# Hybrid mixer of a float32 transformer on one core: heads in pairs, attention inside the projections

## The reference, cut to what matters

```python
h = x @ w_in                                  # 1024 -> 2816
qa, ka, va, qr, kr, vr, gr = split(h)         # 512,128,128,512,512,512,512
qa, ka = apply_rope(qa), apply_rope(ka)       # 8 query heads, 2 key heads of 64
y_attn = sliding_window_sink_attention(qa, ka, va, sinks)   # window 128, blocks of 128
qr, kr = pair_rotation(qr), pair_rotation(kr) * HEAD_DIM ** -0.5
y_ret = multiscale_retention(qr, kr, vr, gr)  # 8 heads: (q k' * decay) v, group norm, silu(gr) gate
return concatenate([y_attn, y_ret]) @ w_out   # 1024 -> 1024
```

## Time and profile before

| | |
|---|---|
| median of three runs | 2790.81 us |
| profiled execution, its own time | 2790.5 us |
| its span | 2788.7 us |
| mean granted TensorE clock | 0.919 |
| busy share of the span: PE, DVE, ACT, POOL | 86%, 34%, 29%, 6% |
| chain that ended last, by engine | PE 79%, DVE 7%, DMA 6%, issue 4%, ACT 3% |
| HBM | 252 GB/s over the span |

### The profile page before, as it was taken

The page is one execution under the profiler, slowest core; times in us unless marked ns, Lnnn a source line. Parts: engine busy times, 40 slices in busy tenths (PEclk is TensorE's granted clock), DMA queues, the critical chain, the costliest instruction groups (busy, mean ns, idle before and its releaser), DMA issues.

```text
span 2788.7 us, 39503 instructions
## 1 busy us (share of the span) xinstructions
PE 2404.5 (86%) x14190; PEld 1708.1 (61%) x14191; DVE 956.3 (34%) x1687; ACT 821.8 (29%) x1357; POOL 166.6 (6%) x274
## 2 busy tenths in 40 slices
PE   5899858888886968888888699998899899988997
PEld 2445523333333963333333699877899899867997
DVE  0223030000002750000000554565554554746554
ACT  1221111111111421111111344443443543443444
POOL 0000001111111001111111000000000000000000
PEclk8899979999998989999999799987999999968999
DMA  9511859999998527999998755422346446222442
GB/s 395 203 58 61 311 216 427 389 427 428 427 409 348 185 106 303 428 427 424 420 415 350 251 175 164 151 77 88 132 156 214 136 154 197 91 90 92 160 150 84
DMA packets 301584, 677.58 MB, mean 243 GB/s; under 512 B 14808, under 2 KB 209368, under 8 KB 259472
## 3 DMA queue, kind: packets, MB, share of 16 engines
q1 hardware_dynamic: 289440, 659.05, 61.2%
q0 software_dynamic: 10720, 8.45, 0.9%
q10 hardware_dynamic: 1296, 8.32, 0.8%
HBM read 682.29 MB, written 20.19 MB: 252 GB/s over the span
## 4 chain that ended last, share of the span: by engine, by line
PE 79%; DVE 7%; DMA 6%; issue 4%; ACT 3%; SPq 1%; POOLq 0%; DVEq 0%; ACTq 0%; POOL 0%
PE ps L1628 28%; PE ps L1078 14%; PE ps L1098 8%; PE ps L1811 5%; DMA ring<-in_moe_w_up 3%; DMA ring<-in_w_mod 3%; DVE arena L1291 1%; PE ps L1089 1%; PE ps L688 1%; PE ps L1079 1%; ACT arena L1155 1%; PE ps L1445 1%; PE ps L1447 1%; PE ps L1446 1%; PE ps L458 1%
## 5 line engine op out<-in xcount | busy, mean ns | idle before, releaser
L1628 PE MATMUL ps<-XS,WS 128*128 128x256 f32 x4224 | 521.0, 287 | 22.8 <-DVE XS L439 22.8
L1628 PEld LDWEIGHTS ps<-XS,WS 128*128 128x128 f32 x4224 | 518.1, 194 | 26.6 <-DVE XS L439 26.4
L1078 PE MATMUL ps<-ring,arena 128*64 128x512 f32 x1040 | 466.4, 602 | 61.0 <-issue 58.1
L1079 PE MATMUL ps<-ring,arena 128*64 128x512 f32 x1040 | 467.9, 603 | 0.0
L1613 DVE TENSOR_TENSOR WS<-ring,WS 128x1024 fp32r<-128x1024 f32 (+1 forms) x276 | 329.5, 1194 | 299.2 <-ACT WS L1608 299.0
L1608 ACT CAST WS<-ring 128x1024 fp32r<-128x1024 f32 (+1 forms) x276 | 282.0, 1023 | 442.9 <-PE ps L1628 420.4
L1078 PEld LDWEIGHTS ps<-ring,arena 128*64 128x64 f32 x1040 | 139.8, 139 | 351.4 <-issue 351.4
L1291 DVE TENSOR_TENSOR arena<-arena,ps 64x512 f32<-64x512 f32 x65 | 44.8, 690 | 851.9 <-ACT arena L1155 851.9
L1098 PE MATMUL ps<-ring,arena 128*64 128x512 f32 x520 | 269.0, 666 | 39.6 <-DVE arena L1294 39.6
L1099 PE MATMUL ps<-ring,arena 128*64 128x512 f32 x520 | 270.8, 670 | 0.0
L1628 PE MATMUL ps<-HS,WS 128*128 128x256 f32 x2112 | 262.2, 285 | 0.0
(11 more groups left out here) (272 smaller groups left out, 2712.3 us busy)
## 6 DMA issues: line engine op xcount, KB each, us to landing
ring<-in_moe_w_gate SPq DMA_DIRECT2D x64, 2048.0 KB, 16.5
ring<-in_moe_w_up SPq DMA_DIRECT2D x64, 2048.0 KB
ring<-in_moe_w_down SPq DMA_DIRECT2D x64, 2048.0 KB, 18.5
ring<-in_ffn_w_gu SPq DMA_DIRECT2D x90, 1024.0 KB, 7.6
ring<-in_w_mod SPq DMA_DIRECT2D x24, 2048.0 KB, 13.5
ring<-in_ffn_w_down SPq DMA_DIRECT2D x32, 1408.0 KB, 6.3
ring<-in_w_in SPq DMA_DIRECT2D x10, 2048.0 KB, 7.7
ring<-in_conv_w_in SPq DMA_DIRECT2D x6, 2048.0 KB, 18.0
```

What stands on the lines that cost most here:

```text
L1078: pe.matmul(ps[0:CAP, 0, :], x, gate[:, j, c, :], start=k == 0, stop=k == KD - 1)
L1079: mm = pe.matmul(ps[CAP:P, 0, :], x, up[:, j, c, :], start=k == 0, stop=k == KD - 1)
L1628: mm = L.eng.matmul(out_ap, weights[:, i, :], moving[:, j, k, :], start=k == 0 and weights is wh and j == 0, stop=k == total - 1 and weigh ...
```

## The change

- Heads lie in pairs on 128 partitions: `QA`, `QT`, `KR` are four tiles of 128x256 each, `KA` holds each key head on both halves. A rotation ends in one addition of 128x256; for `ka` it ends in four of 64x256.
- `ka` is projected first, straight from `XT`; `qa` 0 to 3 follow.
- Attention works on four pairs, inside the steps of the projections. At step i of 21: scores of pair i//4 at i = 3, 7, 11, 15; VectorE's masking there; exponentials at the step after; normalising at i = 5, 9, 13, 17; transposes at 6, 10, 14, 18; probabilities by values at 7, 11, 15, 19. The result is rounded and split straight from PSUM into `YS`.
- Masking, maxima and scaling work on both heads at once, with broadcast operands.
- Gates are copied, and one Silu of 128x1024 follows.
- An output unit is now half the k tiles by 256 output columns: units 20 to 23 are attention's half, 24 to 27 (`B_UNIT`) retention's. Attention's half is computed between the pairs of retention. All eight output tiles stay in four PSUM banks until the end.
- The four reciprocals and the normalising of retention are laced with that half. Retention's k tiles 4 and 5 come as eight output tiles each, then 6 and 7 together.
- The residual is added two tiles at a time. The LayerNorm behind the mixer uses banks 2 and 3, and now splits the feed-forward's unit 3 itself.

TensorE's new order, with the helpers cut:

```diff
+                def scores(p):
+                    L.wait(self.rotated, p + 2)
+                    if p:
+                        L.wait(self.p_kept, p)
+                    for cols, keys in ((slice(0, P), slice(0, P)), (slice(P, 3 * P), slice(0, TL))):
+                        for j in range(2):
+                            queries = slice(0, P) if cols.start == 0 else slice(P, TL)
+                            mm = pe.matmul(self.pair_tile(j)[:, cols], QA[self.heads(j), p, queries], KA[self.heads(j), p // 2, keys],
+                                           start=True, stop=True)
+                    L.inc(mm, self.scores)
...
+                for i in range(5, self.STEPS):
+                    if i < self.VALUE_STEP:
+                        project(i)
+                        turn(i - 1)
+                    elif i < self.GATE_STEP:
+                        retention_values(i - self.VALUE_STEP)
+                        if i == self.VALUE_STEP:
+                            turn(12)
+                    else:
+                        gate(i - self.GATE_STEP)
+                    if i % 4 == 2:
+                        turn_probs(i // 4 - 1)
+                    if i % 4 == 3:
+                        finish(i // 4 - 1)
+                        if i // 4 < self.PAIRS:
+                            scores(i // 4)
...
+                r_scores(0)
+                window_half(0)
+                r_scores(1)
+                r_finish(0)
+                window_half(1)
+                r_scores(2)
+                r_finish(1)
+                mean(0)
+                window_half(2)
+                r_scores(3)
+                r_finish(2)
+                mean(1)
+                variance(0)
+                window_half(3)
+                r_finish(3)
+                mean(2)
+                variance(1)
+                mean(3)
+                variance(2)
+                for k in (4, 5):
+                    L.wait(self.y_split, k + 1)
+                    for m in range(KD):
+                        L.wait(self.w_split, B_UNIT + m // 2 + 1)
+                        y_products(m, k)
+                    if k == 4:
+                        variance(3)
+                for m in range(KD):
+                    for k in (6, 7):
+                        L.wait(self.y_split, k + 1)
+                        mm = y_products(m, k)
```

VectorE's new order:

```diff
+                for i in range(self.STEPS):
+                    if 1 <= i <= self.VALUE_STEP:
+                        rotate(i - 1)
+                    if i % 4 == 3 and i >= 7:
+                        split_out(i // 4 - 1)
+                    if i % 4 == 3 and i // 4 < self.PAIRS:
+                        mask_scores(i // 4)
+                    if i % 4 == 1 and 5 <= i <= 17:
+                        normalise(i // 4 - 1)
+                    if i < self.VALUE_STEP:
+                        if i:
+                            self.split_weights(L, self.unit_of(i) + UNITS)
+                    else:
+                        self.split_weights(L, GATE_UNIT + i - self.VALUE_STEP)
...
+                decay(3)
+                centre(1)
+                gate(0)
+                add_eps(0)
+                self.split_weights(L, B_UNIT + 2)
+                centre(2)
+                gate(1)
+                scale(0)
+                add_eps(1)
+                centre(3)
+                gate(2)
+                scale(1)
+                self.split_weights(L, B_UNIT + 3)
+                split_gated(0)
+                add_eps(2)
+                gate(3)
+                scale(2)
+                split_gated(1)
+                add_eps(3)
+                scale(3)
+                split_gated(2)
+                split_gated(3)
```

More of the change, by code:

```diff
@@ L146 @@
 ACT_PER_LAYER = 0
-DVE_PER_LAYER = 108
+DVE_PER_LAYER = 75
 SPLITS_PER_LAYER = 2 * FFN_UNITS + MIXER_UNITS
@@ L1816, in pe, with project @@
-                stream = [[XS[:, x, k, :] for x in range(2)] for k in range(KD)]
+                    L.inc(mm, self.w_used)
+                def project(i):
+                    if i >= 2:
+                        L.wait(self.raw, i - 1)
+                    if i:
+                        products(self.unit_of(i), self.tile(i), self.x_split if i == 1 else None)
+                        return
+                    slot_ready(L, self.first + 1)
+                    wv = self.weights(1, 256)
+                    for k in range(KD):
+                        L.wait(self.x_high, k + 1)
+                        mm = pe.matmul(self.tile(i), wv[:, k, 0:P], XT[:, k, 0:TL], start=k == 0, stop=k == KD - 1)
+                    L.inc(mm, self.key_tile)
@@ L1818, in turn @@
                 def turn(i):
                     L.wait(self.raw, i + 1)
[L1821 to L1825, removed]
+                    if i:
+                        L.wait(self.rotated, i)
+                    L.inc(pe.matmul(self.turned_tile(), TURN_A if i < 5 else TURN_R, RAW[i % 2], start=True, stop=True), self.turned)
@@ L1848, in pe, with retention_values @@
[L1848 to L1857, removed]
-                    else:
-                        products(self.unit_of(i), ps[:, i % 2, 0:TL], stream, range(KD), self.x_split if i == 0 else None)
+                def retention_values(q):
+                    if q == 0:
+                        L.wait(self.values_kept, 2)
+                    u = VALUE_UNIT + q
+                    L.wait(self.w_split, u + 1)
+                    high_part, low_part = self.parts(u)
+                    for t in range(2):
+                        for i in range(2):
+                            k = 2 * q + i
+                            for weights, x in ((high_part, 0), (high_part, 1), (low_part, 0)):
+                                mm = pe.matmul(ps[:, 5 + t, :], XS[:, x, k, t * P:(t + 1) * P], weights[:, i, :],
+                                               start=k == 0 and x == 0 and weights is high_part,
+                                               stop=k == KD - 1 and weights is low_part)
+                        if t == 0 and q == 3:
+                            L.inc(mm, self.values)
+                    L.inc(mm, self.w_used)
@@ new lines, in gate @@
+                def gate(t):
+                    if t < 2:
+                        L.wait(self.raw, 12 + t)
+                    else:
+                        L.wait(self.gates_kept, t - 1)
+                    products(GATE_UNIT + t, self.tile(13 + t))
+                def scores(p):
[8 more added lines that the diff above has]
+                    L.inc(mm, self.scores)
@@ L1861, in pe @@
+                for i in range(5):
+                    project(i)
                     if i:
                         turn(i - 1)
[L1863 to L1872, removed]
@@ new lines, in r_scores @@
+                def r_scores(m):
+                    if m == 0:
+                        L.wait(self.rotated, 13)
+                        L.wait(self.gates_kept, 4)
+                    else:
+                        L.wait(self.decayed, m)
+                    for cols, keys, queries in ((slice(0, TL), slice(0, P), slice(0, TL)), (slice(TL, 3 * P), slice(P, TL), slice(P, TL))):
+                        for j in range(2):
+                            mm = pe.matmul(ps[:, j, cols], KR[self.heads(j), m, keys], QT[self.heads(j), m, queries],
+                                           start=True, stop=True)
+                    L.inc(mm, self.r_scores)
@@ L1952, in pe, with mean, variance @@
+                def mean(m):
+                    L.wait(self.r_outs_kept, m + 1)
+                    if m == 0:
+                        L.wait(self.p_kept, 4)
+                    else:
+                        L.wait(self.centred, m)
+                    L.inc(pe.matmul(ps[:, 3, 0:TL], HEAD_MEAN, O4[:, m, :], start=True, stop=True), self.means)
+                def variance(m):
                     L.wait(self.squares, m + 1)
+                    L.wait(self.decayed, 4)
                     if m >= 2:
@@ L1983, in act @@
                     scale = HD ** -0.5 if part in ("qa", "kr") else 1.0
-                    L.inc(act.activation(RAW[i % 2], ps[:, i % 2, 0:TL], ACT.Copy, scale=scale), self.raw)
+                    L.inc(act.activation(RAW[i % 2], self.tile(i), ACT.Copy, scale=scale), self.raw)
                     if u is not None:
                         self.round_weights(L, u + UNITS)
-                    if part == "qr" and t == 0:
-                        for t2 in range(2):
-                            L.wait(self.values, t2 + 1)
-                            L.inc(act.copy(VA[:, t2, :], ps[:, 4 + t2, 0:P]), self.values_kept)
@@ L2140, in dve @@
+                for u in range(2, UNITS - 1):
+                    ffns[1].split_weights(L, u)
                 end(L, "dve")
```

531 lines of the change are left out of this document (280 added, 251 removed).

## The result

The changed kernel takes 2697.47 us in the median of four runs, before 2786.83; the ratio is 0.9673, 95% interval 0.9655 to 0.9691. (One of the four, at a mean clock of 0.80, took 2844.4 us and isn't in the ratio; the other three are 2694.33, 2695.7 and 2699.23.) The profiled execution took 2694.33 us, its span is 2692.5. The forecast was 2699.

What follows compares the result with a forecast made beforehand. TensorE was taken to bound the kernel, its clock dipping in the mixer. Per layer 72.9 + 10.7 + 0.6 + 46.6 = 130.8 us against 176.4, saving 91 over two: 2790.5 - 91 = 2699 us, range 2682 to 2712.

Steps and rivals of the forecast that it cites:

- projections without attention: Mixer's projections alone, with `ka` first winning about 1 us: 72.9 us a layer.
- stalls of the steps: Waits in the projection steps with attention inside: put at 0, bounds 0 and 12 us.
- first score to `centre(2)`: From the first retention score, TensorE's work up to `mean(2)`, with VectorE waiting for it: 21 us.
- to k tile 4: After VectorE's scales and splits, k tile 4 may start 28.5 us after the first retention score.
- k tile 4, half clock: Output projection's k tile 4, after 6 to 7 us of idle TensorE, runs at half clock: 5.4 us.
- to the last split: After `variance(3)`, epsilon, root, scale and rounding, retention's last split ends 38.5 us after the first retention score.
- to the centring: After k tiles 6 and 7, last residual and a split, LayerNorm's centring starts 46.6 us after the first retention score.
- The other LayerNorms are not touched: Feed-forwards, other LayerNorms and the first stack, together over 2400 us, keep their time.
- (b): Attention's TensorE work between projections: 2.7 us a pair, including 0.8 for transposes and 0.2 per shape change; 10.7 for four.
- (c): Whether another engine sets the projections' pace: over four steps VectorE needs 14.9 of 15.9 us, ScalarE less; stalls 0.
- Rival 2: Half clock in the retention stretch too: 14 us a layer more, 2727 us; chance 0.13.
- rival 4: Slower than before: small matmuls pull the clock down in the projections as well, 2877 us; chance 0.04.

Runs made afterwards that it cites:

- the reordering: Changed kernel with one unit of attention's output half kept after the first retention pair's scores, three behind the last pair, scales as early as possible: 2678.37 us, ratio 0.9609.
- the variant with the halves last: Changed kernel with attention's half of the output projection moved from between the retention pairs to behind them: 2681.37 us, ratio 0.9616.
- by-head variant: Changed kernel with each pair's score and product matmuls queued all of one head, then all of the other, in attention and retention: 2695.87 us, ratio 0.9674.

## Why the prediction was right

Its own steps, for one layer, with what the trace after shows (us):

| step | said | measured |
|---|---|---|
| projections without attention | 72.9 | 82.6 - 10.0 = 72.6 |
| attention's PE work | 10.7 | 10.0 (period 15.71 less 4 x 3.30, four times) |
| stalls of the steps | 0 | 0 |
| gap behind the last gate | 0.6 | 0.56 |
| first score to `centre(2)` | 21 | 20.8 |
| to k tile 4 | 28.5 | 28.4 |
| k tile 4, half clock | 5.4 | 5.3 |
| to the last split | 38.5 | 38.4 |
| to the centring | 46.6 | 47.9 |
| mixer's first matmul to centring | 130.8 | 131.0 |

The forecast holds by its mechanism and not only by its number: the terms of the sum fit one by one. The experiments test it from both ends. With attention behind the projections, 72 us are given back. The gap ahead of k tile 4 is in half VectorE's reciprocals (their removal), brings the half clock (the filling), and is a matter of order (the reordering).

That the sum meets 131.0 so closely is in part luck: 1.0 us too much in the projections with attention stands against 1.3 too little at the end. Two terms were off. *To the centring*: the sum ran on to tiles 6 and 7 as 48 matmuls in 5.7 us and left out the LayerNorm's mean tiles between them, two groups at 0.68 each; that is about the 1.3 us. *The other LayerNorms are not touched* was wrong for the one behind the mixer: its second mean now runs at full clock, 3.72 us where it took 5.42 (the 16 matmuls at 1909.44, and at 2560.12 before), and feed-forward starts 9.6 us after the centring instead of 11.3. `ka`, which needs only the rounded stream, also starts 0.45 us sooner after the LayerNorm before it. So a layer saves 45.4 + 1.7 + 0.5 = 47.6, two 95; the profiled execution fell by 96.2. The last us is made of 0.6 in the first stack and 2.1 in the two feed-forwards between the mixers (1966.34 to 2374.06 before, 1918.13 to 2323.74 after), less the 1.7 that the mean behind them lost. The forecast thus lies 4.7 us over the profiled execution, 2694.33, because these small gains were put at nothing.

In (b) the transposes are 0.58 for six, not 0.8, which is most of the difference; a change of shape costs about 0.2, as taken. In (c) VectorE's count was 14.9; it is busy 13.5 of the 15.7. Two slips of the prediction change nothing: with full clock throughout, its own terms give 43.6 and not 43.3, and retention's share of 98% in rival 2 is 23.94 of 24 us in the earlier trace rows.

Of the parts of the change, the place of attention is worth up to three quarters of the gain, by the bound above. The rest was won from the first retention score to the centring: 64.1 us before (2495.06 to 2559.20), 47.9 after.

```profile
2495.06 1.22 PE L1918 MATMUL ps<-arena 64*128 64x256 f32 x2 [0.45 <-ACT A L2004]
```

There the pairs, the full clock, the output's half and the laced reciprocals act together. No run has single heads there, or between the projections, so what the pairing gives by itself isn't shown. The output's half during retention, in the order that it has, costs 4 us a layer or more against standing behind.

Rival 2 (half clock in retention too) is refuted by the window at 1.00, rival 4 by 0.98 in the projections. What stays open is why single heads in retention, with TensorE busy 23.9 of 24 us, stayed at 0.50 before, while pairs with little else between them ran at 0.98 behind their first wait in the variant with the halves last (1871.40 to 1880.00), and at 1.00 in its second mixer. The stretch before began at half clock and the pairs' did not; no run had single heads that began at full clock.

## What to carry to other kernels

A chain that hops between three engines is worth hiding in a stretch where TensorE has steady work, even if its own matmuls stay the same; count first whether VectorE's sum over a period stays under TensorE's. Then look at what stands alone behind: filler work placed early hides waits there, but if it delays the engine that will be last, it is better placed later. One stretch of trace, read in both of two equal layers, measured small changes better than the total time did, and it showed where the two layers were not equal.

## What was not expected of the hardware

Float32 matmuls on different halves of the array overlap although all of one head are queued ahead of all of the other: scores 0.86 us in either order, products 1.07 against 0.80. A gap of 2.9 us ahead of k tile 4 still left it at 4.6 us for 24 matmuls, against 3.1 with the gap filled. The length of the gap doesn't set the price by itself: behind the same gap of 5.9 us k tile 4 took 5.4 and 5.5 in the changed kernel's two mixers, 4.5 and 5.5 in the by-head variant's (1890.28 and 2447.03), 5.0 with attention last. And a wait of 2.12 us was followed by half clock in one mixer and by full clock in the other, in one execution.
